# Query projection, dilated attention and output projection in one block of instruction streams

## What is computed

```python
def dilated_attention(xn, w_q, q_norm, w_out, kv_blocks):
    q = (xn @ w_q).reshape(b, s, N_ATT_GROUPS, KV_PER_GROUP, Q_REP, HEAD_DIM)   # 3 groups x 4 heads x 128
    for g, (window, dil) in enumerate(DIL_CONFIGS):                             # dil 1, 4, 16
        qg = rms_norm(q[:, :, g], q_norm[g])
        o, lse = dilated_branch(qg, kv_blocks[g][0], kv_blocks[g][1], window, dil, slopes[g])
        outs.append(o); lses.append(lse)
    wts = jax.nn.softmax(jnp.stack(lses), axis=0)
    o = jnp.sum(wts[..., None] * jnp.stack(outs), axis=0)
    return o.reshape(b, s, ATT_OUT).astype(xn.dtype) @ w_out
```

## Time and profile before

| | us |
|---|---|
| median of 3 runs (1952.85 to 1955.87) | 1952.98 |
| profiled execution, its time | 1958.28 |
| profiled execution, its span | 1956.4 |
| keys and values, transposes to last value product | about 1044 to 1139.6 |
| query projection | 1141.4 to 1245.8 |
| attention | 1246.7 to 1322.5 |
| output projection | 1323.6 to 1352.1 |

### The profile page before, as it was taken

The page is one execution under the profiler, slowest core; times in us unless marked ns, Lnnn a source line. Parts: engine busy times, 40 slices in busy tenths (PEclk is TensorE's granted clock), DMA queues, the critical chain, the costliest instruction groups (busy, mean ns, idle before and its releaser), DMA issues. The chain is left out here.

```text
span 1956.4 us, 20910 instructions
## 1 busy us (share of the span) xinstructions
PE 1809.6 (92%) x7716; PEld 866.5 (44%) x7716; DVE 727.8 (37%) x1394; ACT 499.5 (26%) x757; POOL 106.0 (5%) x164
## 2 busy tenths in 40 slices
PE   7999999996999999999998999798799999999998
PEld 5555666635333333333344654584333333333343
DVE  2667544313343343333412110372343433433341
ACT  3656233311111111111303325442111111111130
POOL 0025700000000000000000000000000000000000
PEclk8999999996999999999999999898799999999999
DMA  7122222244999999999912112103599999999931
GB/s 242 60 64 78 75 78 68 92 191 170 406 421 421 422 421 421 422 421 421 398 49 86 43 51 86 43 1 135 215 422 420 422 421 421 422 421 421 421 145 43
DMA packets 108333, 488.24 MB, mean 250 GB/s; under 512 B 20080, under 2 KB 36976, under 8 KB 56816
## 3 DMA queue, kind: packets, MB, share of 16 engines
q1 hardware_dynamic: 103664, 470.62, 59.8%
q0 software_dynamic: 4608, 16.78, 2.2%
HBM read 475.32 MB, written 12.06 MB: 249 GB/s over the span
## 5 line engine op out<-in xcount | busy, mean ns | idle before, releaser
L1461 PE MATMUL bank<-ring,xT 128*64 128x512 f32 x2048 | 467.0, 600 | 49.5 <-DMA ring<-in_w 49.1
L1461 PEld LDWEIGHTS bank<-ring,xT 128*64 128x64 f32 x2048 | 142.4, 137 | 322.4 <-issue 279.3
L1412 DVE TENSOR_TENSOR H<-H,bank 128x512 f32<-128x512 f32 x240 | 160.2, 687 | 261.2 <-PE bank L1448 261.2
L1485 PE MATMUL bank<-ring,hT 128*64 128x512 f32 x1024 | 226.8, 595 | 0.5 <-ACT hT L1501 0.5
L1448 PE MATMUL bank<-yp,Sb 128*128 128x512 bf16 x720 | 175.9, 380 | 0.0
L1485 PEld LDWEIGHTS bank<-ring,hT 128*64 128x64 f32 x1024 | 70.7, 137 | 133.0 <-issue 128.2
L934 PE MATMUL bank<-ring,ring 128*128 128x512 f32 x288 | 126.4, 593 | 0.3 <-DVE ring L180 0.2
L417 PE MATMUL bank<-ring,ring 128*128 128x512 f32 x256 | 124.7, 595 | 0.0
L1448 PEld LDWEIGHTS bank<-yp,Sb 128*128 128x128 bf16 x720 | 63.3, 98 | 130.1 <-issue 73.0
L1501 ACT ACTIVATE hT<-bank 128x512 f32<-128x512 f32 x32 | 19.1, 597 | 389.5 <-PE bank L1470 389.5
L1399 DVE TENSOR_TENSOR y<-y,yp 128x512 f32<-128x512 f32 x64 | 44.3, 692 | 197.2 <-ACT yp L1510 197.2
(11 more groups left out here) (253 smaller groups left out, 1990.5 us busy)
## 6 DMA issues: line engine op xcount, KB each, us to landing
ring<-in_w SPq DMA_DIRECT2D x192, 2048.0 KB, 26.2
ring<-in_w_heads SPq DMA_DIRECT2D x16, 1024.0 KB, 5.0
ring<-in_w_ple_gate SPq DMA_DIRECT2D x4, 2048.0 KB, 22.2
ring<-in_w_kv SPq DMA_DIRECT2D x3, 2048.0 KB, 19.4
ring<-in_b_w_q SPq DMA_DIRECT2D x3, 2048.0 KB, 9.3
inverses<-T SPq DMA_DIRECT2D x16, 256.0 KB, 4.3
ring<-in_a_w_out SPq DMA_DIRECT2D x2, 2048.0 KB, 7.9
rows<-ring SPq DMA_DIRECT2D x8, 512.0 KB, 5.6
```

Source lines behind the costliest of these rows:

```text
L1412: dve.tensor_tensor(out, out, k.bank[6 + j % 2][:, :], ALU.add).then_inc(s.added, 1)
L1461: last = pe.matmul(out[e * SLOTS:(e + 1) * SLOTS, :], k.xT[:, at, e * SLOTS:(e + 1) * SLOTS], w[:, e, c, :], start=(at == 0), stop=(at == ...
L1485: last = pe.matmul(k.bank[2 + n][e * SLOTS:(e + 1) * SLOTS, :], k.hT[:, c, e * SLOTS:(e + 1) * SLOTS], w[:, e, c % 2, n * HALF:(n + 1) * H ...
```

## The change

The four blocks become one function, `attention`, with one stream per engine, and one barrier at its end. Keys and values are made as before (class `Keys`). The query heads now come in the order head 0 of the groups 0, 1, 2, then head 1 of the groups, and so on, in two banks; the sum of head n-1 stands behind the third product of head n. TensorE makes the first three heads, then runs a loop over b from -2: `turn(b)`, three products, `combine(b)`, three products, `scores(b + 2)`, until the heads are used up at b = 9. From b = 11 on the filling is one product of the output projection at each of the two places. The rest of the output projection follows the loop. Scores and results have one set of banks in place of two; the turned pieces had one before. `aoT`, the copied pieces and the scores lie in the second ring buffer. On ScalarE `exps(b + 2)` now stands behind the output copy b, and squares and roots of the heads are placed by `(b + 2) % 4`.

```diff
-def project_out(k, tag, xT, chunks, slots_of, following):
...
-def head_features(k, tag, gain, w_of, ntiles, out, norm_gain, first_slots, following, values=None, scale=None,
-                  fresh=True):
...
+def square(act, k, s, n, bank):
+    act.wait_ge(s.proj, n + 1)
+    if n >= 2:
+        act.wait_ge(s.sums, n - 1)
+    act.activation(k.sqr[:, n % 2, :], bank[:, :], ACT.Square).then_inc(s.sq, 1)
...
+def root(act, k, s, n, bank):
+    act.wait_ge(s.sums, n + 1)
+    if n >= 2:
+        act.wait_ge(s.out, n - 1)
+    act.activation(k.rnorm[:, n % 2, :], bank[:, :], ACT.Ln, bias=k.eps, scale=1.0 / HD).then_inc(s.ln, 1)
+    act.wait_ge(s.ln, n + 1)
+    act.activation(k.rnorm[:, n % 2, :], k.rnorm[:, n % 2, :], ACT.Exp, scale=-0.5).then_inc(s.rn, 1)
...
+def scaled_head(dve, k, s, n, out, bank, gain):
+    dve.wait_ge(s.rn, n + 1)
+    dve.scalar_tensor_tensor(out, bank[:, :], gain, k.rnorm[:, n % 2, :], ALU.mult, ALU.mult).then_inc(s.out, 1)
...
+    SUMS, FULL, NEAR, TURNED, TURNED_NEAR, OUT = 2, 3, 4, 5, 6, 7
...
+            def sums(n):
+                pe.wait_ge(q.sq, n + 1)
+                wait(pe, q.ln, n)
+                pe.matmul(bank[SUMS][:, :], k.ones, k.sqr[:, n % 2, :], start=True, stop=True).then_inc(q.sums, 1)
...
+            def queries():
+                for n in range(LAST):
+                    g, qh = n % GROUPS, n // GROUPS
...
+                    if n >= 2:
+                        pe.wait_ge(q.out, n - 1)
+                    for c in range(DC):
+                        if n == 0:
+                            norm_chunk(pe, q, c)
+                        last = pe.matmul(bank[n % 2][:, :], w[:, c, :], k.xnT[:, c, :], start=(c == 0),
+                                         stop=(c == DC - 1))
+                        if c == DC - 1:
+                            last.then_inc(q.proj, 1)
+                        if n and c == 2:
+                            sums(n - 1)
+                        yield
+                sums(LAST - 1)
...
+            def early_units():
+                pe.wait_ge(s.w_out, 16)
+                pe.wait_ge(q.out, LAST)
+                pe.wait_ge(s.out, 8)
+                for u in range(3):
+                    yield from unit(u, range(2))
+                pe.wait_ge(s.out, 12)
+                for u in range(3):
+                    yield from unit(u, (2,))
...
             def scores(b):
                 qh, d = blocks[b]
-                kv = qh // 2
-                if b >= 2:
-                    pe.wait_ge(s.biased, 2 * (b - 1))
-                pe.matmul(bank[b % 2][:, :], k.qT[:, qh, d::4], k.kT[:, kv, :], start=True, stop=True)
+                head = qh // 2
+                pe.wait_ge(q.out, GROUPS * (qh + 1))
+                wait(pe, s.biased, 2 * b)
+                pe.matmul(bank[FULL][:, :], k.qT[:, qh, d::4], k.kT[:, head, :], start=True, stop=True)
...
+            def combine(b):
+                pe.wait_ge(s.PTa, b + 1)
+                pe.wait_ge(s.PTb, b + 1)
+                wait(pe, s.out, b)
...
+            keys.tensor(pe)
...
+            pe.wait_ge(kv.out, keys.heads)
+            pe.wait_ge(kv.v, 2 * NT)
+            norm_tensor(pe, k, q, fresh=False)
+            rest = queries()
+            take(rest, GROUPS * DC)
+            for b in range(-2, NB):
+                if b == LAST - 2:
+                    take(rest, 1)
+                if b == LAST - 1:
+                    rest = early_units()
+                filling = 3 if b < LAST - 2 else 1
+                if b >= 0:
+                    turn(b)
+                take(rest, filling)
+                if b >= 0:
+                    combine(b)
+                take(rest, filling)
                 if b + 2 < NB:
                     scores(b + 2)
...
+            for _ in rest:
+                pass
+            pe.wait_ge(s.biased, 2 * NB)
+            for u in (3, 4, 5):
+                for _ in unit(u, range(QPG - 1)):
+                    pass
+            pe.wait_ge(s.out, NB)
+            for u in range(2 * NT):
+                for _ in unit(u, (QPG - 1,) if u < 6 else range(QPG)):
+                    pass
+            for g in range(GROUPS):
+                R.takes[g] += 1
+                R.free[g] = (q.proj, LAST)
...
+            keys.vector(dve)
+            dve.tensor_scalar(k.g_kq[:, 1, :], k.g_kq[:, 1, :], HD ** -0.5, None, ALU.mult).then_inc(q.scaled, 1)
+            norm_vector(dve, k, q, k.g_b, fresh=False)
+            dve.wait_ge(q.scaled, 1)
+            for n in range(GROUPS - 1):
+                scaled(n)
+            dve.wait_ge(*s.dist_landed)
+            for b in range(-2, NB):
+                if b >= 0:
+                    dve.wait_ge(s.turned, b + 1)
+                    wait(dve, s.O, b)
+                    dve.tensor_copy(k.PTb[:, :], bank[TURNED_NEAR][:, 0:2 * P]).then_inc(s.PTb, 1)
+                if -1 <= b < NB - 1:
                     normalise(b + 1)
+                step = GROUPS * ((b + 2) // 4) + 2
+                if step < LAST and (b + 2) % 4 == 0:
+                    scaled(step)
+                elif step + 1 < LAST and (b + 2) % 4 == 1:
+                    scaled(step + 1)
+                elif step + 2 < LAST and (b + 2) % 4 == 3:
+                    scaled(step + 2)
                 if b + 2 < NB:
                     softmax(b + 2)
...
+            norm_scalar(act, k, q, k.g_b, fresh=False)
+            for n in range(GROUPS):
+                square(act, k, q, n, bank[n % 2])
+                if n:
+                    root(act, k, q, n - 1, bank[SUMS])
+            for b in range(-2, NB):
+                if b >= 0:
+                    act.wait_ge(s.turned, b + 1)
+                    wait(act, s.O, b)
+                    act.activation(k.PTa, bank[TURNED][:, :], ACT.Copy).then_inc(s.PTa, 1)
+                step = GROUPS * ((b + 2) // 4) + 2
+                phase = (b + 2) % 4
+                if step < LAST and phase == 0:
+                    root(act, k, q, step, bank[SUMS])
+                elif step + 1 < LAST and phase == 1:
+                    square(act, k, q, step + 1, bank[(step + 1) % 2])
+                if b >= 0:
+                    act.wait_ge(s.O, b + 1)
+                    act.activation(k.aoT[:, blocks[b][0], blocks[b][1]::4], bank[OUT][:, 0:P],
+                                   ACT.Copy).then_inc(s.out, 1)
+                if step + 1 < LAST and phase == 1:
+                    root(act, k, q, step + 1, bank[SUMS])
+                elif step + 2 < LAST and phase == 2:
+                    square(act, k, q, step + 2, bank[(step + 2) % 2])
+                elif step + 3 < LAST and phase == 3:
+                    root(act, k, q, step + 2, bank[SUMS])
+                    square(act, k, q, step + 3, bank[(step + 3) % 2])
                 if b + 2 < NB:
                     exps(b + 2)
             load_sqrt_table(act, k)
...
         @block.sync
         def _(sp):
+            sp.wait_ge(kv.vproj, 2 * NT)
+            load_out(sp, s.w_out, R.landed[5])
             following(sp)
...
+                k.aoT = k.ring2[:, 1, 0:QPG * SEQ].rearrange("p (h n) -> p h n", h=QPG)
+                k.PTa = k.ring2[:, 1, 4096 - SEQ:]
...
+                def prefetch(sp):
+                    for slots in ((4,), (0, 1, 2), (5,), (3,)):
+                        prefetch_experts(sp, k, 1, slots)
...
+                attention(k, load_out, prefetch)
+            end_phase()
```

More of the change, by code:

```diff
@@ L866, in _, with feature_semaphores @@
             following(sp)
-def project_out(k, tag, xT, chunks, slots_of, following):
[L871 to L893, removed]
 NSCORE = SEQ + 2 * P
 NDIST = 3 + SEQ + 2 * P
-def head_features(k, tag, gain, w_of, ntiles, out, norm_gain, first_slots, following, values=None, scale=None,
-                  fresh=True):
+def feature_semaphores(k, tag):
     s = norm_semaphores(k, tag)
@@ L913, in head_features @@
         ("proj", "sq", "sums", "ln", "rn", "out", "scaled", "vproj", "v"))
[L914 to L987, removed]
@@ new lines, in unit @@
+            def unit(u, chunks):
+                n, t = u // NT, u % NT
+                w = R.flat(3).rearrange("p (h n) -> p h n", h=QPG)
+                for c in chunks:
+                    last = pe.matmul(bank[u][:, :], k.aoT[:, c, t * P:(t + 1) * P], w[:, c, n * HALF:(n + 1) * HALF],
+                                     start=(c == 0), stop=(c == QPG - 1), skip_group_check=True)
+                    if c == QPG - 1:
+                        last.then_inc(s.done, 1)
+                    yield
@@ L1041, in scores, with take @@
+            def early_units():
[7 more added lines that the diff above has]
+                    yield from unit(u, (2,))
+            def take(units, n):
+                for _ in range(n):
+                    next(units, None)
             def scores(b):
                 qh, d = blocks[b]
-                kv = qh // 2
@@ L1050, in scores, with turn @@
                 last.then_inc(s.S, 1)
-            scores(0)
```

(23 more changed lines are left out.)

192 lines of the change are left out of this document (96 added, 96 removed).

## The result

The changed kernel took 1978.08 us, the median of 4 runs (1973.17 to 1984.17), against 1954.42 us for the kernel before (4 runs, 1952.85 to 1956.05). The ratio is 1.0113, 95% interval 1.0095 to 1.0132: slower by 23.7 us, where +17.7 was forecast, and inside the range. A second measurement of the same kernel (first experiment) gave 1.0106, or +20.8 us.

A forecast was written before the change was run, and what follows sets the result against it. TensorE bounds the kernel, busy 1809.6 of 1956.4 us. Stalls of 36.9 us replace 23.0 idle, less 1.0 at a barrier: +12.9; the clock adds 4.8: +17.7, so 1970.7 us, range 1960 to 1980.

The forecast's parts named there:

- Removed, and the start: Three barriers go: the one before the query projection saves 1.0 us, idle 8.3 and 3.1 us go; moved loads cost nothing.
- (a) Two banks: Head of the query products: heads 2 and 3 wait for their banks, 11.2 us together; scores(0) wait another 1.1 us.
- (b) The combination behind the next softmax: Attention loop: combinations wait for ScalarE's copy behind the next exps; 1.4 us in the first cycle, 7.0 in two full ones.
- (c) The tail: Last attention blocks: 6.5 us of stalls through scores(12), 7.3 over three blocks of 8.06 us, 2.4 at combine(14).
- (d) The clock: Low clock behind the two 5.6 us stalls at the head of the query products: +4.8 us, bounds 0 and 6.1.
- I take no loss there: Attention's tail: the clock stays up through gaps of up to 3.3 us, so no time is added.
- The sum: Whole change: +12.9 us from stalls less what is removed, +4.8 for the clock, +17.7 us in all.
- No fall of the clock: Rival, head of the query products: the 5.6 us stalls do not lose the clock; +12.9, 1965.9 us; chance 0.20.
- The tail at 1.2 GHz: Rival, attention's tail: repeated idle gaps keep TensorE at the low clock; +37, 1990 us; chance 0.12.
- The covers hold: Rival, attention loop and tail: combinations are ready after turn and three products; -5.3 us, 1947.7 us; chance 0.09.
- Cheap roots: Rival, ScalarE's roots of the heads: no table load before each Ln and Exp; -1.5 us, 1951.5 us; chance 0.04.

The follow-up runs named there:

- e1: Changed kernel with ScalarE rooting head n-1 before squaring head n, for the three heads before the loop: 1964.62 us, ratio 1.0035.
- e7: Changed kernel with a third bank, for head 2, and the order of square and root kept: 1969.98 us, ratio 1.0056.
- e3: Changed kernel with the copies of turned block b+1 ahead of exps and softmax of block b+2, on ScalarE and VectorE: 1962.02 us, ratio 1.0020.
- e0: The changed kernel measured again, unedited, as the base for the other runs: 1979.1 us, ratio 1.0106.
- e6: Changed kernel with products nobody reads filling TensorE's waits in the tail, and two waits to protect banks in use: 1975.11 us, ratio 1.0079.
- e5: Changed kernel with six products nobody reads in each of the two long waits at the head of the query products: 1972.38 us, ratio 1.0070.
- e4: Changed kernel with the edits of e1 and e3 together: 1948.55 us, ratio 0.9952.
- e8: e4 with each group's last head rooted before the exps and scaled before the normalisation, and two output products ahead of scores(12): 1943.73 us, ratio 0.9928.
- e9: Kernel before, barriers and banks kept, with scores(b+2) behind combination b and exps(b+2) behind output copy b, no filling: 2014.74 us, ratio 1.0297.

## Why the prediction was right, and where its size was off

**Removed, and the start.** Right. The barrier of 1.8 us became a wait of 0.9, 0.9 saved for a forecast 1.0; the 8.3 and the 3.1 went as such. The moved loads cost nothing that the waits show.

**(a) Two banks.** Right as a size: 5.58 and 5.41 us for two of 5.6, and 1.00 for 1.1 ahead of the first scores. Its name was half the story: the stall needs both halves, a bank that is written again two heads later and a root that stands behind the next head's square. e1 keeps two banks and has no stall; e7 keeps the order, has three banks and keeps one stall.

**(b) The combination behind the next softmax.** Right. Counted between the starts of turns (1223.64, 1234.91, 1245.44, 1255.80, 1265.59) the phases took 11.27, 10.53, 10.36 and 9.79 us, for 11.3, 10.64, 10.47 and 9.91; a cycle 41.95 for 42.3, so the two cycles cost 0.7 us less than forecast. e3 shows the cause: the copies ahead of the exps and the softmax take the waits of L1086 from 15.2 us in e0 (14.0 in the first trace) to 0.7.

**(c) The tail.** The chain was right: scores(12) end with the turn at 1318.87, 11.3 us after the scores before them (1307.55), as forecast, and the first block took 7.96 us for 8.06. From the last scores to the end it took about 28.9 us, for 28.8.

**(d) The clock.** At the head: 5.25 + 4.33 - 2 x 2.57 = 4.4 us on the six passes, 4.9 with what follows them, for +4.8. That close a hit is partly luck. The middle of the bounds stood for two equal falls; one cost 3.1 us, the upper bound, the other 1.8, near the lower, and in e0 they cost 1.9 and 2.9. Nor was the 5.0 us of idle time ahead of a fall a fixed length: it was 4.9 and 5.4 us here, 2.5 and 4.1 us in e0. In the tail "I take no loss there" is **the step that failed**. The clock fell three times. The first fall was hidden in the next wait, the other two made blocks of 9.62 and 9.65 us out of 8.06: 3.1 us, and e6, which fills those waits, gave back 3.1. The argument had been one gap of 3.1 us behind which the clock stayed up. The same trace held the opposite case, the wait of 2.9 us for the first softmax: the clock, back at 0.96 in 1250 to 1252, fell again inside it, and the work behind it ran at 0.50.

```profile
1252.00:1254.00 2.00, 0.00 (x0) 0.00 (x0) 1.93 (x6) 1.01 (x3) 0.00 (x0) 0.90 0.00 0
1254.00:1256.00 2.00, 1.37 (x7) 1.37 (x8) 0.57 (x1) 0.91 (x2) 0.00 (x0) 0.50 0.00 0
...
1254.63 1.54 PE L1061 MATMUL bank<-consts,sc 128*128 128x128 f32 x6 [2.89 <-DVE sc L1104]
```

So a gap of some 3 us had kept the clock once and lost it once, and "no loss" had no firm ground. The tail has gaps of 1.0 to 3.1 us again and again. By the rule cited in the prediction (the Trainium skill, "TensorE: Matmul & The Clock Gate", "Why this matters for your kernels": no gap over about 3 us) the gap ahead of scores(12) would have cost 2.4 us, nearer than my zero in size. But the two falls that reached the end of the stage came behind waits of 2.19 us, which that rule lets pass, and the gap that it does name cost nothing in the end. That rule lets the 2.89 us gap pass as well, and the clock fell in it.

**The sum.** +17.7 + 3.1 (tail's clock) - 0.7 (cycles) is +20.1, for +20.5 measured in the stage. The medians give +23.7, the ratio measured again +20.8. Of the 6.0 us between the forecast's +17.7 and the medians' +23.7 the stage explains 2.8. For the other 3.2 no cause is shown; with them the 1978.08 us lie close to the upper end of the range, 1980. Both intervals (18.6 to 25.8, and 17.0 to 24.5) hold the stage's 20.5, and the first does not hold 17.7.

**The rivals.** *No fall of the clock*: out, by the windows 0.50 behind both long waits, and e5. *The tail at 1.2 GHz*: right that it falls there, wrong in size; the clock fell at three places of the tail and came back within the block each time, and the cost was 3.1 us and not 19. *The covers hold*: out, by 14.0 us of waits at L1086. In e3 and e4, where the copy comes first, they do hold. *Cheap roots*: out; L904 and L906 have a load before each of their 12 activations in the stage, 24 in all.

Not tried: the removal of the barriers alone. The likely reading, that merging the blocks gains and the order inside costs more, rests on e4 and e8, which keep everything but the order and are faster than the kernel before. It stays a reading.

## What to carry to other kernels

When two stages are interleaved, write down for each in-order engine what stands between an input's arrival and its use; an instruction that TensorE waits for goes ahead of work for the block after it. Here two such swaps, of equal instructions, were worth 30 us, and turned 1.1% slower into 0.5% faster. Price the clock for short waits too, above all where they repeat, and not only for the one long idle; look for a row that speaks against the one you argue from; and look again for what is late next once a chain has been shortened.

## What the runs showed of the hardware that was not expected

The granted clock fell at short waits: three times in the tail of the changed kernel (waits of 3.1, 2.19 and 2.19 us), and once in the kernel before (2.89 us). Equal waits did not end alike. In the tail the third wait of 2.19 us, ahead of 1349.98, kept the clock (1.00 in 1350 to 1352); in the kernel before the gap of 3.1 us kept it. In e9 waits of 3.05 us stood ahead of the combinations at 1294.14 and 1301.36: behind the first the clock stayed at 1.00, behind the second it fell soon after (0.66 in 1302 to 1304, then 0.50). And in e0, the same kernel again, the falls stood at other blocks, yet its tail lost about as much: from turn(10) to the end of the stage e0 took 71.4 us and the first trace 71.6, for 68.2 in e6. So such a loss can be bounded from these runs, but not counted per wait.

Whether the spread of the executions comes from these falls is not shown. The changed kernel's runs spread over 11.0 and 12.5 us and those of e5 and e6 over 4.0 and 4.6, but the kernel before spread over 3.2 us in 4 runs and over 11.3 us in the 17 beside e0.
